# Scores, values and turning of an attention step at one point among the dense products instead of two

## The chip, the cores and the metric

The kernel runs on one core of one Trainium2 chip. The metric is the device time of one execution in microseconds (us); less is better. Engines are named as in the profile: PE is TensorE's matmuls, PEld its weight loads, DVE is VectorE, ACT is ScalarE, POOL is GpSimd, and SP issues DMAs.

## The reference

One decoder layer over 1024 tokens of width 1024, in float32. The input is normalised and multiplied by one wide matrix; the columns feed a sliding-window attention with a sink logit per head, an mLSTM, and several gates; the two branches are projected, gated, summed, projected again and added to the input. What matters here is the attention, with 16 query heads in 4 groups that share a key/value head, and blocks of 128 tokens:

```python
h = rms_norm(x, norm_w)
proj = jnp.einsum('btd,de->bte', h, w_in) + b_in
...
scores = jnp.einsum('bnqkgd,bnskd->bnkgqs', qb, kw).astype(jnp.float32) * (ATTN_HEAD_DIM ** -0.5)
...
probs = jax.nn.softmax(jnp.concatenate([scores, sink], axis=-1), axis=-1)[..., :-1]
out = jnp.einsum('bnkgqs,bnskd->bnqkgd', probs.astype(v.dtype), vw)
```

## The kernel before

**Dense work.** The wide projection is cut into pairs of weight tiles. Each pair costs seven products instead of eight (a Strassen-like scheme), and each product is 12 matmuls of 128x512 (PRODUCT = 12, PAIR = 84), issued at L1036. The weights are split in a high and a low part (ring_hi by ACT at L1396, ring_lo by POOL at L799). A finished product is taken out of PSUM by ACT and DVE in the functions called retire, which wait for it.

**Attention among it.** attention_step(g) handles one group of four heads, g = 0 to 3, and carries 3 pairs, so 252 dense matmuls, with it. Inside it n runs over 0 to 9. Block n's work is spread over three steps:

- scores(n): 8 matmuls at L1123, at the first point of step n;
- turning of block n: 4 transposes of the probabilities at L1172, in step n + 1;
- values of block n: 4 or 8 matmuls at L1165 and L1167, in step n + 2.

The order is written out by hand, engine by engine; semaphores join the engines. PE issues dense matmuls up to a position, then attention work. The positions are

```python
return LEAD + (3 * PAIR - LEAD - TAIL) * (2 * n + half) // (2 * NB + 2)
```

which for half 0 gives 12, 37, 62, 88, 113, 138, 164, 189, 214, 240 for n = 0 to 9, and for half 1 gives 24, 50, 75, 100, 126, 151, 176, 202, 227 for n = 0 to 8.

**The softmax chain of block n.** PE does scores(n). ACT copies the part of the current block to probs (L1596). DVE's combine(n) merges the previous block's part (L2191; L2194 for n = 0), takes the row maxima (L2197, L2200) and gives neg_max (L2203). ACT does four exponentials and the sink's (L1599, L1601). DVE's normalise(n) sums, inverts and scales (L2208, L2210, L2212, and last L2214, which writes probs). PE then turns the block (waits for probs_ready), DVE's select masks the turned block into pT_cur and pT_prev (L2222, L2224), PE multiplies by the values (waits for pT_ready), and for n under 3 ACT copies the result to u_early (L1609), for the others DVE's gate multiplies it into silu_z (L2236).

DVE also does silu of the z gate (L2230) after normalise in steps 4, 5 and 7, and the retired products (L2091 to L2115).

Of the kernel before, what the change touches and what calls it, by code (L numbers as in the profile page):

```python
# [9 lines left out]
ACT = mybir.ActivationFunctionType  # L10
# [3 lines left out]
P = 128  # L14
# [3 lines left out]
NB = T // P  # L18
# [85 lines left out]
def attention_at(n, half):  # L104

    return LEAD + (3 * PAIR - LEAD - TAIL) * (2 * n + half) // (2 * NB + 2)
# [8 lines left out]
def build(nc, x, norm_w, w_in, b_in, sinks, conv_w, conv_b, mnorm_w, wba, wbm, w_out, fnorm_w, out):  # L115
    ctx = ExitStack()
    with ctx:
# [809 lines left out]
        def _(pe):  # L927
# [199 lines left out]
            def attention_step(g):  # L1127
                i0 = 1 + 3 * g
                done = [0]

                def more(hi):

                    pairs(i0, done[0], hi)
                    done[0] = hi

                for n in range(NB + 2):
                    more(attention_at(n, 0))
                    if n < NB:
                        if n == 0:
                            pe.wait_ge(k_in, 32 * (g + 1))  # L1140
                            pe.wait_ge(c11_out, i0)
                            pe.wait_ge(c12_out, i0)
                            if not later(g):
                                pe.wait_ge(g_ready, 1)
                        else:
                            pe.wait_ge(cur_copied, NB * g + n)
                            pe.wait_ge(max_ready, NB * g + n)
                        scores(n).then_inc(scores_done, 1)
                    if n <= NB:
                        more(attention_at(n, 1))  # L1150
                    if n >= 2:
                        m = n - 2
                        pe.wait_ge(pT_ready, NB * g + m + 1)
                        if m == 0:
                            pe.wait_ge(v_in, 16 * (g + 1))
                        if m == 0 and later(g):
                            pe.wait_ge(attn_gated, (NB - EARLY) * g)
                        if 1 <= m <= EARLY:
                            pe.wait_ge(attn_copied, EARLY * g + m)
                        if m > EARLY:  # L1160
                            pe.wait_ge(attn_gated, (NB - EARLY) * g + m - EARLY)
                        for r in range(2):
                            o = ps[64 * r:64 * r + 64, X[3], 0:2 * P]
                            heads = slice(2 * r, 2 * r + 2)
                            mm = nc.tensor.matmul(o, v_head[:, m, :], pT_cur[:, heads, :], start=True, stop=(m == 0))  # L1165
                            if m:
                                mm = nc.tensor.matmul(o, v_head[:, m - 1, :], pT_prev[:, heads, :], start=False, stop=True)  # L1167
                        mm.then_inc(pv_done, 1)
                    if 1 <= n <= NB:
                        pe.wait_ge(probs_ready, NB * g + n)  # L1170
                        for h in range(GR):
                            mm = nc.tensor.transpose(ps[:, X[2], h * P:(h + 1) * P], probs[(n - 1) % 2][:, h, :], ident[:])  # L1172
                        mm.then_inc(probs_turned, 1)
                more(3 * PAIR)
# [170 lines left out]
        def _(act):  # L1345
# [187 lines left out]
            def attention_step(g):  # L1533
# [55 lines left out]
                for n in range(NB + 2):  # L1589
                    retire(attention_at(n, 0))  # L1590
                    if n < NB:
                        pr = probs[n % 2]
                        act.wait_ge(scores_done, NB * g + n + 1)
                        if n >= 2:
                            act.wait_ge(probs_turned, NB * g + n - 1)
                        A(pr[:], both_blocks[:, :, 1, :], ACT.Copy).then_inc(cur_copied, 1)  # L1596
                        act.wait_ge(max_ready, NB * g + n + 1)
                        for h in range(GR):
                            A(pr[:, h, :], pr[:, h, :], ACT.Exp, scale=HD ** -0.5, bias=neg_max[:, h:h + 1],  # L1599
                              accum_out=row_sum[:, h:h + 1])  # L1600
                        A(sink_exp[:], sink_in[:], ACT.Exp).then_inc(exp_ready, 1)  # L1601
                    if n == NB and not final(g, KV):
                        load_k(g + 1)
                    if 2 <= n < EARLY + 2:
                        m = n - 2
                        act.wait_ge(pv_done, NB * g + m + 1)
                        if m == 0:
                            until(act, early_used, g)
                        A(u_early[:, :, m * P:(m + 1) * P], ps[:, X[3], 0:2 * P].rearrange("p (j n) -> p j n", j=2),  # L1609
                          ACT.Copy).then_inc(attn_copied, 1)  # L1610
                    if n <= NB:
                        retire(attention_at(n, 1))
                    if n in (3, 4):
# [379 lines left out]
        def _(dve):  # L1993
# [149 lines left out]
            def attention_step(g):  # L2143
# [94 lines left out]
                for n in range(NB + 2):  # L2238
                    retire(attention_at(n, 0))
                    if n < NB:  # L2240
                        combine(n)
                    if n <= NB:
                        retire(attention_at(n, 1))
                    if 1 <= n <= NB:
                        select(n - 1)
                    if n >= EARLY + 2:
# [1 line left out]
                    if n == NB + 1:  # L2248
                        dve.drain()
                        dve.sem_inc(u_ready, 1)  # L2250
                    if n < NB:
                        normalise(n)
                    if n == 4:
# [415 lines left out]
```

## Time and profile before

| | us |
|---|---|
| median of 3 runs | 1123.01 (1122.79 to 1123.10) |
| the profiled execution | 1122.33 |
| its span in the trace | 1120.6 |
| PE busy | 1100.2 |
| DVE busy | 777.9 |
| ACT busy | 483.3 |
| POOL busy | 641.3 |

The span is what the trace covers; the profiled execution's own time is 1.7 us more. PE is busy nearly all of the span. The four attention groups begin with their first scores at 96, 176, 256 and 336 us. The granted TensorE clock is 0.999 of full speed.

### The profile page before, as it was taken

Reading aid. Unit: us, or ns where it says so; the run is one execution under the profiler, and the core shown is the slowest. Engines: PE = TensorE matmul, PEld = TensorE weight load, DVE = VectorE, ACT = ScalarE, POOL = GpSimd, SP = SyncE. Lnnn points to the kernel's source line nnn. Section 1 sums busy time; section 2 is a strip of 40 time slices with the busy share of each in tenths; the row PEclk is TensorE's granted clock in tenths of the full one; section 3 lists DMA queues with packets and bytes.
Section 4 is the critical chain, followed back from the end, with each engine's and each line's share of the span. In section 5 each row is a group of like instructions: output and inputs, shape, how many; then the busy total and the mean of one; then the engine's idle time right before and its main releaser. Section 6 shows DMA issues by size and latency. Waiting matters only on the chain.

```text
span 1120.6 us, 16419 instructions
## 1 busy us (share of the span) xinstructions
PE 1100.2 (98%) x5363; PEld 877.0 (78%) x5363; DVE 777.9 (69%) x1235; ACT 483.3 (43%) x1134; POOL 641.3 (57%) x441
## 2 busy tenths in 40 slices
PE   6999999999999999999999999999999999999997
PEld 5887777777777778888888888888887888788876
DVE  4966887887878887567756675669578312458897
ACT  7543443534434444454535364545455311131443
POOL 3577455465565469556955695659644434347440
PEclk9999999999999999999999999999999999999999
DMA  6244133142151141112311222122109433853423
GB/s 211 78 86 83 39 94 94 29 117 72 37 149 36 39 136 38 38 39 85 104 38 39 77 88 61 37 75 85 48 20 336 160 104 106 268 167 136 167 93 134
DMA packets 112804, 107.63 MB, mean 96 GB/s; under 512 B 7228, under 2 KB 96696, under 8 KB 111720
## 3 DMA queue, kind: packets, MB, share of 16 engines
q1 hardware_dynamic: 102760, 77.18, 23.2%
q10 hardware_dynamic: 9984, 29.69, 8.5%
q8 instruction: 33, 0.54, 0.2%
q14 instruction: 27, 0.22, 0.1%
HBM read 80.50 MB, written 26.35 MB: 95 GB/s over the span
## 4 chain that ended last, share of the span: by engine, by line
PE 79%; DVE 9%; ACT 4%; DVEq 3%; DMA 2%; issue 2%; ACTq 1%; SPq 0%; POOL 0%; POOLq 0%
PE ps L1036 50%; PE ps L1265 13%; PE ps L942 3%; PE ps L1123 2%; DMA w_raw<-in_w_branch_mlstm 1%; PE ps L1239 1%; PE ps L1223 1%; PE ps L1227 1%; PE ps L1236 1%; PE ps L1165 1%; DVE row_max L2197 1%; PE ps L1172 1%; DVEq L2259 1%; ACT ring_hi L1396 1%; DVE v L2427 1%
## 5 line engine op out<-in xcount | busy, mean ns | idle before, releaser
L799 POOL TENSOR_TENSOR ring_lo<-w,ring_hi 128x512 fp32r<-128x512 f32 x128 | 178.7, 1413 | 136.3 <-ACT ring_hi L1396 136.3
L799 POOL TENSOR_TENSOR ring_lo<-t,ring_hi 128x512 fp32r<-128x512 f32 x96 | 136.3, 1424 | 143.0 <-ACT ring_hi L1396 143.0
L1036 PE MATMUL ps<-s_hi,ring_hi 128*128 128x512 f32 x512 | 203.5, 397 | 0.0
L1036 PE MATMUL ps<-s_lo,ring_hi 128*128 128x512 f32 x512 | 202.6, 396 | 0.0
L1036 PE MATMUL ps<-s_hi,ring_lo 128*128 128x512 f32 x512 | 202.0, 395 | 0.0
L1036 PE MATMUL ps<-h_hi,ring_hi 128*128 128x512 f32 x384 | 152.1, 396 | 0.0
L1036 PE MATMUL ps<-h_hi,ring_lo 128*128 128x512 f32 x384 | 151.9, 396 | 0.0
L1036 PE MATMUL ps<-h_lo,ring_hi 128*128 128x512 f32 x384 | 151.4, 394 | 0.0
L1396 ACT ACTIVATE ring_hi<-w 128x512 fp32r<-128x512 f32 x128 | 75.6, 620 | 93.4 <-PE ps L1036 78.4
L1036 PEld LDWEIGHTS ps<-s_hi,ring_hi 128*128 128x128 f32 x512 | 96.2, 188 | 22.1 <-issue 3.0
L1036 PEld LDWEIGHTS ps<-s_hi,ring_lo 128*128 128x128 f32 x512 | 96.3, 188 | 21.8 <-issue 2.6
L1036 PEld LDWEIGHTS ps<-s_lo,ring_hi 128*128 128x128 f32 x512 | 96.3, 188 | 19.7 <-issue 1.3
L1599 ACT ACTIVATE probs<-probs,neg_max 128x128 f32<-128x128 f32 x128 | 49.9, 391 | 111.2 <-DVE neg_max L2203 111.2
L794 POOL TENSOR_TENSOR t<-w,t 128x512 f32<-128x512 f32 x64 | 94.4, 1475 | 5.1 <-issue 5.1
L782 POOL TENSOR_TENSOR w_hi<-w_raw,zero_col 128x1024 fp32r<-128x1024 f32 (+1 forms) x18 | 37.2, 2065 | 101.2 <-PE ps L1265 58.9
L1036 PEld LDWEIGHTS ps<-h_hi,ring_hi 128*128 128x128 f32 x384 | 72.2, 188 | 16.8 <-issue 1.3
L1036 PEld LDWEIGHTS ps<-h_hi,ring_lo 128*128 128x128 f32 x384 | 72.2, 188 | 15.4 <-issue 1.3
L1036 PEld LDWEIGHTS ps<-h_lo,ring_hi 128*128 128x128 f32 x384 | 72.2, 188 | 15.3 <-issue 1.3
L1396 ACT ACTIVATE ring_hi<-t 128x512 fp32r<-128x512 f32 x96 | 59.3, 623 | 53.8 <-PE ps L1036 46.6
L1265 PE MATMUL ps<-u_a,w_hi 128*128 128x512 f32 x256 | 79.1, 390 | 0.3 <-DVE u_a L2432 0.3
L1814 ACT ACTIVATE ev<-ev 128x1024 f32<-128x1024 f32 x16 | 17.0, 1062 | 110.5 <-DVE merged L2509 49.4
L1265 PE MATMUL ps<-u_m,w_hi 128*128 128x512 f32 x192 | 59.9, 393 | 0.4 <-POOL w_lo L784 0.4
(331 smaller groups left out, 2318.9 us busy)
## 6 DMA issues: line engine op xcount, KB each, us to landing
w<-in_w_in SPq DMA_DIRECT2D x128, 256.0 KB, 3.0
xs<-in_x SPq DMA_DIRECT2D x8, 512.0 KB, 8.3
ga_scratch<-ev ACTq DMA_DIRECT2D x4, 1024.0 KB, 4.8
u_scratch<-silu_z ACTq DMA_DIRECT2D x8, 512.0 KB, 3.4
gm_scratch<-ev ACTq DMA_DIRECT2D x4, 1024.0 KB, 4.8
w_raw<-in_w_branch_attn SPq DMA_DIRECT2D x8, 512.0 KB, 4.1
u_a_f<-u_scratch SPq DMA_DIRECT2D x4, 1024.0 KB, 8.2
ev<-ga_scratch ACTq DMA_DIRECT2D x8, 512.0 KB, 3.5
```

The source lines that it names most:

```text
L782: nc.gpsimd.tensor_tensor(hi, src, zero_col[:].to_broadcast(list(src.shape)), ALU.add)
L794: return nc.gpsimd.tensor_tensor(flat(dst), flat(a), flat(b), op)
L799: return nc.gpsimd.tensor_tensor(flat(lo[:]), flat(raw_or_sum[:]), flat(hi[:]).bitcast(F32), ALU.subtract)
L942: mm = nc.tensor.matmul(ps[:, 2 * s + b, :], w[:, k, :], h[:, k % KH, :], start=(r == 0), stop=(r == KT * TERMS - 1))
L1036: mm = nc.tensor.matmul(ps[:, bank, :], w[:, k, :], h[:, k, :], start=(m == 0), stop=(m == PRODUCT - 1))
L1123: mm = nc.tensor.matmul(o, q_T[rows, j, n * P:(n + 1) * P], k_now[rows, first * P:(n + 1) * P], start=True, stop=True)
L1165: mm = nc.tensor.matmul(o, v_head[:, m, :], pT_cur[:, heads, :], start=True, stop=(m == 0))
L1172: mm = nc.tensor.transpose(ps[:, X[2], h * P:(h + 1) * P], probs[(n - 1) % 2][:, h, :], ident[:])
L1265: mm = nc.tensor.matmul(ps[:, 2 * s + b, :], w[:, k, :], part(k)[(0, 1, 0)[term]][:, token_half(b)], start=(r == 0), stop=(r == KT * TERMS ...
L1396: return A(ring_slot[0][:], raw_or_sum[:], ACT.Copy)
L1599: A(pr[:, h, :], pr[:, h, :], ACT.Exp, scale=HD ** -0.5, bias=neg_max[:, h:h + 1], accum_out=row_sum[:, h:h + 1])
L1814: A(ev[:, j, :], ev[:, j, :], ACT.Tanh, scale=0.5).then_inc(gate_tanh, 1)
```

## The change

On PE the dense matmuls that stood between scores(n) and the values and turning are no longer issued there; they follow in the next step's first run of dense matmuls. So a step has one point for all attention work, at position half 0, and runs of 25 or 26 dense matmuls between the points. ACT's copy of the early values comes ahead of the exponentials, and DVE retires the second product of a step after select and gate.

```diff
--- before.py
+++ after.py
@@ -1146,8 +1146,6 @@
                             pe.wait_ge(cur_copied, NB * g + n)
                             pe.wait_ge(max_ready, NB * g + n)
                         scores(n).then_inc(scores_done, 1)
-                    if n <= NB:
-                        more(attention_at(n, 1))
                     if n >= 2:
                         m = n - 2
                         pe.wait_ge(pT_ready, NB * g + m + 1)
@@ -1594,6 +1592,14 @@
                         if n >= 2:
                             act.wait_ge(probs_turned, NB * g + n - 1)
                         A(pr[:], both_blocks[:, :, 1, :], ACT.Copy).then_inc(cur_copied, 1)
+                    if 2 <= n < EARLY + 2:
+                        m = n - 2
+                        act.wait_ge(pv_done, NB * g + m + 1)
+                        if m == 0:
+                            until(act, early_used, g)
+                        A(u_early[:, :, m * P:(m + 1) * P], ps[:, X[3], 0:2 * P].rearrange("p (j n) -> p j n", j=2),
+                          ACT.Copy).then_inc(attn_copied, 1)
+                    if n < NB:
                         act.wait_ge(max_ready, NB * g + n + 1)
                         for h in range(GR):
                             A(pr[:, h, :], pr[:, h, :], ACT.Exp, scale=HD ** -0.5, bias=neg_max[:, h:h + 1],
@@ -1601,13 +1607,6 @@
                         A(sink_exp[:], sink_in[:], ACT.Exp).then_inc(exp_ready, 1)
                     if n == NB and not final(g, KV):
                         load_k(g + 1)
-                    if 2 <= n < EARLY + 2:
-                        m = n - 2
-                        act.wait_ge(pv_done, NB * g + m + 1)
-                        if m == 0:
-                            until(act, early_used, g)
-                        A(u_early[:, :, m * P:(m + 1) * P], ps[:, X[3], 0:2 * P].rearrange("p (j n) -> p j n", j=2),
-                          ACT.Copy).then_inc(attn_copied, 1)
                     if n <= NB:
                         retire(attention_at(n, 1))
                     if n in (3, 4):
@@ -2239,8 +2238,6 @@
                     retire(attention_at(n, 0))
                     if n < NB:
                         combine(n)
-                    if n <= NB:
-                        retire(attention_at(n, 1))
                     if 1 <= n <= NB:
                         select(n - 1)
                     if n >= EARLY + 2:
@@ -2248,6 +2245,8 @@
                     if n == NB + 1:
                         dve.drain()
                         dve.sem_inc(u_ready, 1)
+                    if n <= NB:
+                        retire(attention_at(n, 1))
                     if n < NB:
                         normalise(n)
                     if n == 4:
```

On PE, at step 1 of a group, the first point at which a block is turned, the difference of the two orders reads as follows (a minus stands before, a plus in the change; L1170 is the old L1172):

```order
 L1123 MATMUL ps<-k_now,q_T 128x256 [waits max_ready,cur_copied]
 L1123 MATMUL ps<-k_now,q_T 128x256 x3
+L1170 MATMUL ps<-ident,probs_159 128x128 [waits probs_ready]
+L1170 MATMUL ps<-ident,probs_159 128x128 x3
 L1036 MATMUL ps<-s_lo,ring_hi 128x512
 L1036 MATMUL ps<-s_hi,ring_lo 128x512
```

The four transposes, with their wait for probs_ready, moved ahead of 13 dense matmuls, to right behind the scores of the next block.

On DVE, in step 4 of the first group, before (ev is the buffer that the retired product goes to):

```order
L2203 TENSOR_SCALAR neg_max<-row_max 128x4
L2096 SCALAR_TENSOR_TENSOR ev<-ps,par,ev 128x512
L2222 TENSOR_TENSOR pT_cur<-ps,cur_T 128x512
L2224 TENSOR_TENSOR pT_prev<-ps,prev_T 128x512
L2208 TENSOR_TENSOR row_inv<-row_sum,sink_exp 128x4
```

and in the same place of the change, whose line numbers are one less:

```order
L2202 TENSOR_SCALAR neg_max<-row_max 128x4
L2221 TENSOR_TENSOR pT_cur<-ps,cur_T 128x512
L2223 TENSOR_TENSOR pT_prev<-ps,prev_T 128x512
L2095 SCALAR_TENSOR_TENSOR ev<-ps,par,ev 128x512
L2207 TENSOR_TENSOR row_inv<-row_sum,sink_exp 128x4
```

The retired product moved behind the two masked copies; both still stand between combine and normalise.

## Rows read from the trace of the kernel before

**Rows 1.** Page, busy us (share of the span) and instructions

```profile
PE 1100.2 (98%) x5363; PEld 877.0 (78%) x5363; DVE 777.9 (69%) x1235; ACT 483.3 (43%) x1134; POOL 641.3 (57%) x441
```

**Rows 2.** Chain that ended last: start us, us, what; first group, step 1

```profile
102.71 1.06 PE ps L1123 x8
103.77 3.17 PE ps L1036 x13
106.95 0.44 PE ps L1172 x4
107.38 2.75 PE ps L1036 x12
```

**Rows 3.** The same view, first group, steps 5 to 8

```profile
145.62 2.94 PE ps L1036 x12
148.56 0.59 PE ps L1165 x4
149.15 0.43 PE ps L1167 x4
149.58 0.59 PE ps L1172 x4
150.17 2.99 PE ps L1036 x13
...
159.00 5.71 PE ps L1036 x25
```

**Rows 4.** Timeline (start us, us, engine, line): scores(1), end of normalise(0)

```profile
102.64 0.73 PEld L1123 LDWEIGHTS ps<-k_now,q_T 64*128 64x128 f32 x8 [0.35 <-issue]
103.43 1.65 DVE L2214 TENSOR_TENSOR probs<-probs,row_inv 128x512 f32<-128x512 f32 x1
```

**Rows 5.** Timeline, second group: scores(1), end of normalise(0), combine(2)

```profile
182.56 0.73 PEld L1123 LDWEIGHTS ps<-k_now,q_T 64*128 64x128 f32 x8 [0.35 <-issue]
184.12 1.78 DVE L2214 TENSOR_TENSOR probs<-probs,row_inv 128x512 f32<-128x512 f32 x1
193.45 0.72 DVE L2191 COPY_PREDICATED probs<-from_prev,ps 128x512 f32<-128x512 int8 x1
```

**Rows 6.** One line's instructions: L2214, duration ns min/median/max

```profile
L2214 DVE TENSOR_TENSOR probs<-probs,row_inv x32: 691/1417/1784, 103.4 to 404.1; 128x512 f32<-128x512 f32 x32
```

**Rows 7.** Timeline: end of normalise(7) in groups 0 to 3

```profile
162.49 1.77 DVE L2214 TENSOR_TENSOR probs<-probs,row_inv 128x512 f32<-128x512 f32 x1
...
242.50 1.78 DVE L2214 TENSOR_TENSOR probs<-probs,row_inv 128x512 f32<-128x512 f32 x1
...
322.32 1.54 DVE L2214 TENSOR_TENSOR probs<-probs,row_inv 128x512 f32<-128x512 f32 x1
...
404.06 1.77 DVE L2214 TENSOR_TENSOR probs<-probs,row_inv 128x512 f32<-128x512 f32 x1
```

**Rows 8.** Timeline, weight loads: values of block 7 in groups 0 to 3

```profile
169.31 0.23 PEld L1165 LDWEIGHTS ps<-pT_cur,v_head 128*64 128x64 f32 x4 [0.41 <-DVE pT_prev L2224]
...
249.36 0.20 PEld L1165 LDWEIGHTS ps<-pT_cur,v_head 128*64 128x64 f32 x4 [0.54 <-DVE silu_z L2236]
...
329.23 0.20 PEld L1165 LDWEIGHTS ps<-pT_cur,v_head 128*64 128x64 f32 x4 [0.35 <-DVE silu_z L2236]
...
410.87 0.23 PEld L1165 LDWEIGHTS ps<-pT_cur,v_head 128*64 128x64 f32 x4 [1.78 <-DVE pT_prev L2224]
```

**Rows 9.** Timeline, weight loads: turning of block 7 in the last group

```profile
405.89 0.42 PEld L1172 LDWEIGHTS ps<-ident,probs 128*128 128x128 f32 x4 [0.67 <-DVE probs L2214]
```

**Rows 10.** Timeline, ACT: around the early copy of step 3, and a copy that PE released

```profile
127.01 0.36 ACT L1609 ACTIVATE u_early<-ps 128x256 f32<-128x256 f32 x1
...
145.67 0.60 ACT L1596 ACTIVATE probs<-ps 128x512 f32<-128x512 f32 x1 [0.69 <-PE ps L1123]
```

**Rows 11.** Timeline, DVE, first group: first instruction of combine(4) and combine(7)

```profile
130.77 0.75 DVE L2191 COPY_PREDICATED probs<-from_prev,ps 128x512 f32<-128x512 int8 x1 [1.60 <-ACT probs L1596]
...
156.41 0.74 DVE L2191 COPY_PREDICATED probs<-from_prev,ps 128x512 f32<-128x512 int8 x1 [0.93 <-ACT probs L1596]
```

## The prediction

> **What bounds the kernel now.** I read the page first: PE is busy 1100.2 of 1120.6 us [rows 1], so any microsecond that PE waits is added and any that it saves is taken off, unless something else holds it. Then the chain of waits inside one attention group, which gives the pitch of PE's work. A run of 25 dense matmuls behind a turning takes 5.71 us, of 13 behind a turning 2.99, of 12 behind scores 2.94 [rows 3]; 13 behind scores take 3.17 and 12 behind the turning of step 1 take 2.75 [rows 2]. Each weight load of scores has 0.35 us of idle before it that nothing released [rows 4]: PE pays for a change between kinds of matmul. Last I read DVE's timeline beside PE's. The last instruction of the softmax chain, L2214, ends shortly before or even after PE wants the block, and in the last group PE already waits 0.67 us for it [rows 9]. So inside a group a second, serial chain runs just ahead of PE: combine, exponentials, normalise, then the next combine. It waits for ACT's copies at places [rows 11], which wait for ACT's own earlier work, and hardly for PE.
>
> **The change, part by part.**
>
> *What PE saves.* In steps 2 to 7 the dense matmuls came in two runs, 12 behind scores and 13 behind a turning: 2.94 + 2.99 = 5.93 us. Now 25 come in one run behind a turning: 5.71 [rows 3]. That is 0.22 us a step, 1.32 for six. In step 1 the old pieces are 1.06 + 3.17 + 0.44 + 2.75 = 7.42 [rows 2], the new ones 1.06 + 0.59 + 5.71 = 7.36, with the 0.59 that a turning takes behind another kind of matmul [rows 3]. Together 1.38 a group, 5.5 us for four. Scores followed directly by values stand nowhere in the trace. I price that boundary as dense to values, which the 0.22 assumes; from below it could cost nothing, from above the idle 0.35 [rows 4] more, 24 times: 8.4 us. I take the middle way of no difference, since below it will turn out that PE isn't what ends a group.
>
> By the idle of 0.35 us alone a group would save six of them and all four 24, 8.4 us. The Trainium skill, TensorEngine Tiling (Array Packing), Key Properties, says that changing the tiling mode drains TensorE; scores, values and dense matmuls have different tile shapes and the change has 24 fewer such switches, so by that rule the change gains. The run lengths above say 0.22 for each rather than 0.35, because the idle is partly time that the pipeline would have taken anyway.
>
> *What PE now waits for: step 1.* The turning of block 0 needs L2214 of normalise(0). It used to stand behind 13 dense matmuls (3.17 us); now it stands directly behind scores(1). In group 0 scores(1) start at 102.64, so PE is free for the turning at 103.70; L2214 ends at 103.43 + 1.65 = 105.08 [rows 4]. With 0.06 us from the end of L2214 (404.06 + 1.77 = 405.83) to the turning (405.89) [rows 7, 9] PE stands 1.44 us. In group 1: free at 182.56 + 1.06 = 183.62, L2214 ends at 184.12 + 1.78 = 185.90 [rows 5], so 2.34 us. Nothing can fill it: PE issues in order, and the dense matmuls are queued behind the turning. Nothing in step 0 is changed on ACT or DVE, so this chain isn't shorter. This alone is more than the 1.38 that a group saves, but it isn't what to add up, for the following reason.
>
> *What ends a group: block 7.* From the turning of block 0 PE alone would need: five runs of 25 with the turning ahead, 0.59 + 5.71 = 6.30 each; two runs of 26 (positions 62 to 88 and 138 to 164), 6.53 each; scores and four value matmuls once, 1.06 + 0.59 = 1.65; scores and eight value matmuls (0.59 + 0.43 = 1.02) five times, 2.08 each; values alone, 1.02, in step 8 [rows 2, 3]. The sum is 31.50 + 13.06 + 1.65 + 10.40 + 1.02 = 57.63. In group 0 that is 105.14 + 57.63 = 162.77 for the turning of block 7. L2214 of normalise(7) ends at 162.49 + 1.77 = 164.26 [rows 7]. So PE waits again, about 1.5 us. In group 1: 185.96 + 57.63 = 243.59 against 244.28: 0.7. In the last group PE waited here already with 13 more dense matmuls ahead [rows 9]. So in every group block 7's L2214 sets the time, and behind it PE now has a run of 26 (214 to 240) where it had 13. The values of block 7 can start 0.06 + 0.59 + 5.94 = 6.59 us behind the end of L2214. (5.94 is 5.71 and one more of 0.23; 0.59 is the turning.)
>
> Against what they do now [rows 7, 8]:
> group 0: 164.26 + 6.59 = 170.85, now 169.31: +1.54;
> group 1: 244.28 + 6.59 = 250.87, now 249.36: +1.51;
> group 2: 322.32 + 1.54 + 6.59 = 330.45, now 329.23: +1.22;
> group 3: 405.83 + 6.59 = 412.42, now 410.87: +1.55.
> The sum is +5.82 us, if DVE's chain from a group's first scores to L2214 of block 7 stays as long as it is.
>
> *Does that chain stay?* DVE's instructions are the same; the retired product of a step only goes behind the masked copies, still between combine and normalise. The product is long finished: in step 7 it ends at position 192, three dense matmuls into a run, and DVE comes to it some 4 us after the turning. Two small terms. ACT's copy of the early values (L1609, 0.36 us [rows 10]; instructions of ACT overlap a little at their ends, and I take 0.27) leaves the stretch between the exponentials and ACT's next copy for a place where ACT waits for DVE. ACT's copy of step 4 is what combine(4) waits for, 1.60 us [rows 11]; so 0.27 off in groups 0, 2, 3. And PE's late turning moves scores(2): in group 1 they start at 185.96 + 6.30 = 192.26, ACT copies 1.18 later (145.67, scores from 144.56 less the 0.07 by which the two views differ [rows 3, 10]; 1.06 of it the scores) and for 0.60, DVE follows 0.15 after: 194.19 against 193.45 now [rows 5], so +0.74 - 0.27 = +0.47 there. In the other groups the same sum comes out before DVE gets there. Together -0.81 + 0.47 = -0.34.
>
> *Edits that cost nothing:* ACT's and DVE's retiring frees PSUM banks three products later, 36 dense matmuls or over 8 us, and moves by 2 us at most; POOL and SP have no line changed. Without that cover a late bank would stop PE at the start of a product, which no row shows now.
>
> **Sum.** 1122.33 (the profiled execution, 0.68 under the median) + 5.82 - 0.34 = 1127.8 us. I leave the 0.68 out.
>
> **Rivals.**
>
> *Forecast: the chain ends each group.* Chance 0.76.
>
> *Faster: PE's saving comes through.* The place is L2214 of block 0 and block 7 in each group. It would have to end 1.4 to 2.3 us earlier in block 0 and 0.7 to 1.5 earlier in block 7. For it: the same instruction on the same shape takes from 0.69 to 1.78 us, median 1.42 [rows 6], so up to 1.1 us of one could go when POOL's work falls elsewhere. Against it: block 0's step is not changed at all, and in group 0 nothing ahead of it is. If all waits vanished the kernel would be 5.5 us faster, 1116.8. It decides from about 1.4 us a group: with less saved than that in waits the gain is gone. Chance 0.06. The Trainium skill, SBUF — State Buffer, Who interferes with whom, says that a VectorE tensor_tensor with both inputs in SBUF contends with GpSimd's reads, one blocking the other; L2214 has both inputs there. No row of mine separates this from other causes of the spread.
>
> *No change: only block 0 waits.* If block 7's chain ends in time, because ACT's copy that combine(7) waits for 0.93 us [rows 11] comes sooner, the waits are those of block 0 only: 1.44 and 2.34 by rows, say 1.3 on average with the other two groups shorter, 5.2 in all, against 5.5 saved: 1122.0. Chance 0.11.
>
> *Worse: the chain gets longer itself.* Each PE wait shifts the next scores, hence ACT's copy, hence combine, as I found in group 1 with 0.74. If that happens in all steps from 1 to 7 with some 0.3 us, a group ends 2 us later than forecast: +8, 1136. Chance 0.07.
>
> **How the numbers follow.** Likeliest 1127.8. The range 1122.5 to 1132.5 reaches down to the case of no change and up over half of the worse case; the bound of L2214, 0.7 us on average to either side in each group, gives 2.8 of it. Two runs differ by 0.03%; 0.2%, 2.2 us, is about what tells a change from none. Faster 0.06, same 0.12, slower 0.82.
>
> **What would show it.** In the profile after: PE's idle put to L2214 (probs_ready) at the turning of block 0 and of block 7 in every group, 1 to 2.5 us each, some 10 us in all; groups' first scores 81 to 82 us apart instead of 80; runs of 25 dense matmuls of 5.71 us; fewer gaps of 0.35. From the last group's end to the end of the span nothing changed. The prediction is wrong if L2214 of block 7 ends at another distance from the group's first scores than now, 68.2 us in group 0, or if scores to values costs PE much more than dense to values.

## The result, and the profile after

The change runs in 1129.44 us (median of 6 runs, 1127.31 to 1131.89), the kernel before in 1123.07 beside it (6 runs, 1122.79 to 1123.97). The ratio is 1.0057, 95% interval 1.0042 to 1.0071: slower by 0.57%. Forecast were 1127.8, with 1122.5 to 1132.5 as the range, and slower with a chance of 0.82. The forecast cost was 5.48 us; the medians differ by 6.4.

The profiled execution of the change took 1131.89 us, the longest of its six, with a span of 1130.2. The page's first line, which answers to [rows 1]:

```profile
PE 1098.2 (97%) x5363; PEld 881.4 (78%) x5363; DVE 777.4 (69%) x1235; ACT 486.8 (43%) x1134; POOL 645.1 (57%) x441
```

PE is busy 2.0 us less in a span that is 9.6 longer. The chain that ended last (start us, us, what) shows what took PE's place in the first group and at the start of the second. L1170 is the turning, L1163 and L1165 are the values, L2213 is the old L2214, L2209 the old L2210:

```profile
106.92 1.65 DVE probs L2213
...
109.27 5.71 PE ps L1036 x25
114.98 1.09 PE ps L1123 x8
...
121.45 1.15 DVE row_inv L2207
...
122.67 1.17 DVE row_inv L2209
...
124.16 1.44 DVE probs L2213
...
126.30 5.70 PE ps L1036 x25
...
165.96 1.77 DVE probs L2213
...
168.43 5.94 PE ps L1036 x26
...
187.53 1.26 DVE row_inv L2209
...
189.11 1.76 DVE probs L2213
...
191.74 7.16 PE ps L1036 x25
```

In [rows 2, 3] the same stretches of the first group were PE's alone. Now DVE's L2213 stands between two runs of dense matmuls, and block 7's, at 165.96, stands right ahead of the run of 26 that leads to the group's end. The last run of 25 shown took 7.16 us where the others take 5.71; the last section comes back to it.

The view of waits at L1170 (engine, line, releaser: us, times, longest):

```profile
PEld ps L1170 <- DVE probs L2213: 17.0, 14, 2.6
...
PE ps L1170 <- DVE probs L2213: 10.9, 13, 2.2
```

The waits over 0.8 us at the weight load are blocks 0 and 7 of the four groups, which were forecast, and block 2 of the four groups (0.85 to 1.23 us) and block 6 of the last (1.38), which weren't. Some of them in the timeline of weight loads:

```profile
108.61 0.42 PEld L1170 LDWEIGHTS ps<-ident,probs 128*128 128x128 f32 x4 [0.99 <-DVE probs L2213]
...
125.64 0.42 PEld L1170 LDWEIGHTS ps<-ident,probs 128*128 128x128 f32 x4 [0.86 <-DVE probs L2213]
...
167.77 0.42 PEld L1170 LDWEIGHTS ps<-ident,probs 128*128 128x128 f32 x4 [1.57 <-DVE probs L2213]
...
190.92 0.42 PEld L1170 LDWEIGHTS ps<-ident,probs 128*128 128x128 f32 x4 [2.62 <-DVE probs L2213]
...
251.30 0.42 PEld L1170 LDWEIGHTS ps<-ident,probs 128*128 128x128 f32 x4 [1.18 <-DVE probs L2213]
...
405.21 0.42 PEld L1170 LDWEIGHTS ps<-ident,probs 128*128 128x128 f32 x4 [1.38 <-DVE probs L2213]
...
413.98 0.42 PEld L1170 LDWEIGHTS ps<-ident,probs 128*128 128x128 f32 x4 [1.85 <-DVE probs L2213]
```

The time is read group by group, from a group's first scores to the values of block 7. First the first scores before, in the timeline of weight loads:

```profile
96.10 0.52 PEld L1123 LDWEIGHTS ps<-k_now,q_T 64*128 64x128 f32 x8 [0.36 <-issue]
...
176.03 0.52 PEld L1123 LDWEIGHTS ps<-k_now,q_T 64*128 64x128 f32 x8 [0.35 <-issue]
...
256.08 0.52 PEld L1123 LDWEIGHTS ps<-k_now,q_T 64*128 64x128 f32 x8 [0.35 <-issue]
...
335.96 0.52 PEld L1123 LDWEIGHTS ps<-k_now,q_T 64*128 64x128 f32 x8 [0.35 <-issue]
```

Then the change, first scores and values of block 7 of the four groups:

```profile
100.31 0.52 PEld L1123 LDWEIGHTS ps<-k_now,q_T 64*128 64x128 f32 x8 [0.36 <-issue]
...
174.30 0.20 PEld L1163 LDWEIGHTS ps<-pT_cur,v_head 128*64 128x64 f32 x4 [0.35 <-issue]
...
181.03 0.52 PEld L1123 LDWEIGHTS ps<-k_now,q_T 64*128 64x128 f32 x8 [0.35 <-issue]
...
257.81 0.20 PEld L1163 LDWEIGHTS ps<-pT_cur,v_head 128*64 128x64 f32 x4 [0.35 <-issue]
...
264.53 0.52 PEld L1123 LDWEIGHTS ps<-k_now,q_T 64*128 64x128 f32 x8 [0.35 <-issue]
...
338.11 0.20 PEld L1163 LDWEIGHTS ps<-pT_cur,v_head 128*64 128x64 f32 x4 [0.35 <-issue]
...
344.83 0.52 PEld L1123 LDWEIGHTS ps<-k_now,q_T 64*128 64x128 f32 x8 [0.35 <-issue]
...
420.49 0.20 PEld L1163 LDWEIGHTS ps<-pT_cur,v_head 128*64 128x64 f32 x4 [0.35 <-issue]
```

Before, the groups took 73.21, 73.33, 73.15 and 74.91 us (values in [rows 8]). Now they take 73.99, 76.78, 73.58 and 75.66: +0.78, +3.45, +0.43, +0.75, together +5.41. From the last values to the end of the span it is 709.73 before and 709.71 now. The remaining 4.2 us of the profiled execution lie ahead of the first scores, where nothing is changed: ACT waited 5.81 us for a store of v (3.01 in the profiled execution of before), POOL for ACT, and PE 2.76 us for POOL's ring_lo, at 95.86. In medians the change is 6.4 us slower, 1.0 more than the groups' +5.41.

The late start reached into the first group. There the maximum of block 0 with the sink, line L2200 before and L2199 in the change, reads in the timeline of DVE, before and then in the change:

```profile
99.69 0.87 DVE L2200 SCALAR_TENSOR_TENSOR row_max<-row_max,sink_tab 128x4 f32<-128x4 f32 x1
...
103.89 0.16 DVE L2199 SCALAR_TENSOR_TENSOR row_max<-row_max,sink_tab 128x4 f32<-128x4 f32 x1
```

Before, it started while a POOL instruction ran (99.25 to 100.55). So L2213 of block 0 ends 8.25 us behind the first scores and not 8.99, though no line of this stretch was changed. Of the twelve traces that have L2213 or its like (no_scale and before_no_scale don't), in two, the change and change_silu_late, PE stood over 2 us just ahead of the first scores, and the distance is 8.25 and 8.27 us; in the ten others it is 8.99 to 9.04. One of these is step8_late (below), the same program up to step 8: 9.01 us, and 68.14 instead of 67.41 to the end of block 7's L2213, while its other three groups repeat the change's within 0.03. So, as an estimate from the two traces, the first group of a usual execution of the change is 0.73 us longer than the profiled one, and the groups' loss +6.14 us, close to the medians' 6.4.

### The profile page after: what moved, and what is told of

Same layout as the page of the kernel before. It is cut to its first block, busy times and chain, and to the rows that moved or that the text cites. A ratio compares the mean times of both kernels' runs of the same rounds, so it can differ in the third digit from the quotient of the medians.

```text
span 1130.2 us, 16419 instructions
## 1 busy us (share of the span) xinstructions
PE 1098.2 (97%) x5363; PEld 881.4 (78%) x5363; DVE 777.4 (69%) x1235; ACT 486.8 (43%) x1134; POOL 645.1 (57%) x441
## 4 chain that ended last, share of the span: by engine, by line
PE 67%; DVE 16%; ACT 5%; DMA 4%; DVEq 4%; issue 3%; ACTq 1%; POOL 0%; SPq 0%; POOLq 0%
PE ps L1036 43%; PE ps L1263 13%; DVE probs L2213 2%; DVE row_max L2196 1%; DMA w_raw<-in_w_branch_mlstm 1%; DVE probs L2190 1%; PE ps L1237 1%; PE ps L1221 1%; DVE row_inv L2209 1%; PE ps L1225 1%; PE ps L1234 1%; ACT ring_hi L1394 1%; DMA v_scratch<-v_stage 1%; ACT probs L1594 1%; ACT probs L1605 1%
## 5 line engine op out<-in xcount | busy, mean ns | idle before, releaser
L799 POOL TENSOR_TENSOR ring_lo<-w,ring_hi 128x512 fp32r<-128x512 f32 x128 | 181.3, 1435 | 148.2 <-ACT ring_hi L1394 148.2
```

The source lines that it names most:

```text
L799: return nc.gpsimd.tensor_tensor(flat(lo[:]), flat(raw_or_sum[:]), flat(hi[:]).bitcast(F32), ALU.subtract)
```

## The experiments

All times are medians; the ratio is against the kernel before, run beside them (medians 1123.24, 1123.07, 1123.07). "Groups" is what the four groups of the profiled execution took, less the 294.60 of before.

| kernel | us | ratio [95%] | groups |
|---|---|---|---|
| the change | 1129.44 | 1.0057 [1.0042, 1.0071] | +5.41 |
| step1_late | 1127.40 | 1.0035 [1.0021, 1.0048] | +5.07 |
| step8_late | 1123.84 | 1.0004 [0.9995, 1.0013] | +1.92 |
| values_early | 1121.92 | 0.9986 [0.9977, 0.9995] | -1.48 |
| no_scale | 1114.92 | 0.9923 [0.9910, 0.9937] | -8.19 |
| before_no_scale | 1120.78 | 0.9982 [0.9973, 0.9991] | -2.01 |
| orders_only | 1127.56 | 1.0045 [1.0031, 1.0058] | +3.00 |
| values_early_silu_late | 1119.49 | 0.9970 [0.9960, 0.9980] | -3.70 |
| change_silu_late | 1125.35 | 1.0020 [1.0011, 1.0029] | +1.75 |
| dve_order_only | 1126.46 | 1.0029 [1.0018, 1.0040] | +2.60 |
| act_order_only | 1123.36 | 1.0002 [0.9993, 1.0011] | +0.15 |
| pe_and_act_order | 1132.47 | 1.0082 [1.0068, 1.0096] | +9.82 |
| pe_order_only | 1130.36 | 1.0059 [1.0045, 1.0073] | +7.54 |

The groups and the medians agree within 1.5 us everywhere, mostly within 1. The groups are one execution, and the two executions with the late start (the change, change_silu_late) show 0.73 us too little in the first. orders_only and dve_order_only lose another 1.5 and 1.1 us behind the last values (711.22 and 710.82 us to the end, against 709.73).

**Step 1 undone (step1_late).** If the wait at block 0 is itself the cost, this gives it back; if block 7's chain ends the group, it gives nothing. The diff is against the change, as are all but where it is said.

```diff
                         scores(n).then_inc(scores_done, 1)
+                    if n in (1,):
+                        more(attention_at(n, 1))
...
                         combine(n)
+                    if n in (1,):
+                        retire(attention_at(n, 1))
```

> The change with one step undone: in step 1 the turning of block 0 stands behind 13 dense matmuls again. Theory A (a group ends when block 7's L2214 ends, which hangs on the serial chain of ACT and DVE alone): PE's wait of 1.0 to 2.6 us for block 0 goes, but the wait for block 7 grows by nearly as much; only the slow stretch behind the long wait of the second group (about 1.6 us in the profiled run) and its late scores(2) go. 1126 to 1128 us. Rival B (PE's waits add up, each on its own): the waits for block 0 are taken off and the others stay as they are, 1129.4 - 5.7 - 1.6 = about 1122 us.

Measured 1127.40; the groups stay at +5.07. The wait went one block on, in the timeline of weight loads:

```profile
115.04 0.42 PEld L1172 LDWEIGHTS ps<-ident,probs 128*128 128x128 f32 x4 [1.99 <-DVE probs L2215]
...
166.49 0.42 PEld L1172 LDWEIGHTS ps<-ident,probs 128*128 128x128 f32 x4 [1.60 <-DVE probs L2215]
```

115.04 is block 1 and 166.49 block 7. The four groups take 75.18, 74.43, 73.98 and 76.08 us, against 73.99, 76.78, 73.58 and 75.66 in the change. So the third and fourth are 0.4 us longer without the wait at block 0, and the first too when its late start is allowed for: there that wait isn't what costs. In the second it is, by 2.35 us, since the wait of 2.22 us brings the slow run of 7.16 us with it (last section); here PE's waits stay at 1.54 us and less in the groups, and the clock at 1.00. That this slow stretch would go is what theory A expected. The waits for block 7, which it expected to grow, are the same within 0.1 us; the waits stand at block 1 instead (0.77 to 1.54 us of PE's idle).

**Step 8 undone (step8_late).** The same edit with `n in (8,)`: the values of block 7 are then 13 dense matmuls behind its turning, not 26.

> The change with one step undone: in step 8 the values of block 6 and the turning of block 7 stand behind 13 dense matmuls again, so behind the turning there is a run of 13, not 26. The waits for block 0 stay. Theory A: block 7's L2214 ends when it did, but 13 fewer dense matmuls (3.0 us) stand behind it; the next values then wait for DVE's gate of block 6 and come about 5.0 us behind the end of L2214 instead of 6.6: 1.5 us a group, about 6 us off the change, 1122.5 to 1124.5 us. Rival B: PE only waits less for block 7, by its 1.2 to 1.8 us in each group, and pays one more gap: 1124 to 1126 us; rival C (block 0 is what counts): hardly below the change, 1128 to 1130 us.

Measured 1123.84. In the first group block 7's turning (166.70) and values (170.27) wait for nothing:

```profile
166.70 0.42 PEld L1172 LDWEIGHTS ps<-ident,probs 128*128 128x128 f32 x4 [0.39 <-issue]
170.27 0.21 PEld L1165 LDWEIGHTS ps<-pT_cur,v_head 128*64 128x64 f32 x4 [0.35 <-issue]
```

In the four groups the values of block 7 come 5.38, 5.79, 5.82 and 5.05 us behind the end of L2215 instead of 6.56 to 6.59: 4.3 us less in all, not the 6 of theory A, and they don't wait for the gate, as it had thought. The median falls by 5.6 of the 6.4 us; the 1.3 between isn't traced. All waits for block 0 are still there (1.79 and 2.63 us in the first two groups). What is left in the groups, +1.92, comes from the second (+2.68); the other three together are 0.76 us shorter than before.

**Scores and values together, turning apart (values_early).** One boundary less on PE, and the turning keeps 12 to 13 dense matmuls behind the scores; DVE in the order of before.

```diff
                         mm.then_inc(pv_done, 1)
+                    if n <= NB:
+                        more(attention_at(n, 1))
                     if 1 <= n <= NB:
                         pe.wait_ge(probs_ready, NB * g + n)
```

(and DVE's second retire back ahead of select)

> Scores and values stand at the first point of a step, the turning alone at the second; ACT's early copy ahead of the exponentials as in the change, DVE's retiring where it was before. The L2214 of a block has its old 13 dense matmuls of cover again, and a turning between dense runs pays no gap. By PE's pieces a step costs 1.06 + 1.02 + 3.17 + 0.44 + 2.75 = 8.44 us instead of 8.59: 3.6 us off before in all, 1119.5, if PE alone counts (rival B). Theory A: PE's waits of the change vanish, but a group still ends with DVE's chain, which is as long as before: 1121.5 to 1123.5 us, with PE's idle at the values of block 7 grown instead.

Measured 1121.92, a little faster than before, and in theory A's range. The values of block 7 wait instead of its turning, as in the second group here, which keeps part of PE's saving from coming through:

```profile
249.09 0.20 PEld L1163 LDWEIGHTS ps<-pT_cur,v_head 128*64 128x64 f32 x4 [1.04 <-DVE silu_z L2237]
```

**The chain shortened (no_scale, before_no_scale).** Both leave out the scaling of the probabilities by row_inv; no_scale does so in the change, before_no_scale in the kernel before.

```diff
-                    V.reciprocal(row_inv[:], row_inv[:])
-                    dve.drain()
-                    V.tensor_tensor(pr[:], pr[:], row_inv[:].unsqueeze(2).to_broadcast([P, GR, P]), ALU.mult)\
-                        .then_inc(probs_ready, 1)
+                    V.reciprocal(row_inv[:], row_inv[:]).then_inc(probs_ready, 1)
```

> The change with L2213, the last instruction of normalise, left out: the probabilities aren't scaled, and probs_ready comes from the reciprocal ahead of it. The serial chain is 0.7 to 1.8 us shorter for each of eight blocks. Theory A: nearly all waits of PE at the turning vanish and PE's saving comes through: 1116.5 to 1118.5 us, 5 to 6 us below before. Rival D (what the change costs lies on PE itself, at the new boundary from scores to values, or in dense runs that are longer): the time stays above before, 1126 us or more.

> The kernel before with L2214, the last instruction of normalise, left out: the probabilities aren't scaled. By the before trace PE waits for the chain of DVE only about 4 us in all (groups' ends), so Theory A: 1118.5 to 1121.5 us, and the change with the same left out (1114.92) stays below it by the 5.5 us that its shorter PE work was priced at, or by 4 to 6. Rival D (the change costs PE itself something): 1114.9 or less.

1114.92 and 1120.78. With the chain 0.7 to 1.8 us shorter in each block, the order of the change is 5.9 us faster than that of before. Its groups took 71.60, 71.60, 71.60 and 71.61 us: PE alone sets them. Those of before_no_scale took 73.15, 73.14, 73.15 and 73.15. So the change saves PE 1.55 us a group, 6.2 in all, and loses it to the chain. This leaves no room for a cost on PE itself at the new boundary. no_scale is 1.6 us under the expected range: PE saves 0.7 us more than I had priced, and the 2.0 us of waits that the groups of before still have (294.60 against 292.59) go as well.

**ACT's and DVE's new orders without PE's (orders_only).** Here the positions on PE are those of before.

```diff
                         scores(n).then_inc(scores_done, 1)
+                    if n <= NB:
+                        more(attention_at(n, 1))
```

> The order of ACT and DVE of the change, PE's order of before. Theory A: nothing that PE waits for in a step moves by more than some 0.3 us; DVE's masked copies come 0.7 to 1.5 us ahead of where they were, but must wait for the turning at the second point: 1121.5 to 1124.5 us. If ACT's or DVE's new order were the cause, it would lie near the change's 1129.

The expectation failed: 1127.56, 4.5 us slower than before by orders that I had called free. Two groups of lines of orders_only (line engine op, count; busy, mean ns; idle before, releaser):

```profile
L2223 DVE TENSOR_TENSOR pT_cur<-ps,cur_T 128x512 f32<-128x512 f32 x32 | 22.0, 686 | 3.2 <-PE ps L1172 3.0
...
L2211 DVE TENSOR_SCALAR row_inv<-row_inv 128x4 f32<-128x4 f32 x32 | 18.8, 586 | 2.9 <-issue 0.6
```

DVE now waits 3.0 us for the turning ahead of the masked copies, and the short multiplication of row_inv takes 586 ns in the mean; before, the same line took

```profile
L2210 DVE TENSOR_SCALAR row_inv<-row_inv 128x4 f32<-128x4 f32 x32 | 13.2, 413 | 2.9 <-issue 0.6
```

**The two orders one by one.** dve_order_only, act_order_only and orders_only have PE's order of before, pe_order_only and pe_and_act_order that of the change. The edit in question on DVE is

```diff
-                    if n <= NB:
-                        retire(attention_at(n, 1))
                     if 1 <= n <= NB:
                         select(n - 1)
...
+                    if n <= NB:
+                        retire(attention_at(n, 1))
                     if n < NB:
                         normalise(n)
```

> The kernel before with DVE's order alone: the second product of a step is retired behind the masked copies and the gate. The orders of ACT and DVE together cost 4.5 us on PE's old order, which I had not expected; in its trace the masked copies wait 3.0 us in all for the turning and L2211, a short tensor_scalar, takes 18.8 us in all instead of 13.2. If DVE's order is the cause: 1126 to 1128 us. If ACT's early copy is: 1122.5 to 1123.5 us here.

> The kernel before with ACT's order alone: the early copy of steps 2 to 4 comes ahead of the exponentials and waits for values that PE's old order gives only at the second point. If DVE's order is the cause of the 4.5 us: 1122.5 to 1124 us here; if this wait is: 1125 to 1127.5 us.

> The change with DVE's order of before: the second product of a step is retired ahead of the masked copies. With PE's new order a turning is long done when DVE comes to the masked copies, so the wait that DVE's order costs on PE's old order can't be there, and by theory A only how L2213's and L2209's long forms fall can differ: 1126 to 1130 us. If DVE's order costs its 3 to 4 us here too, 1124.5 to 1126 us.

> The change on PE alone, ACT and DVE as before. Theory A: the same chain ends each group: 1126.5 to 1130.5 us, within 1.5 us of the version with ACT's order too, since that moves one copy of 0.36 us by some 2 us. If the change's cost came from ACT's or DVE's orders: at most 1124 us.

ACT's order changes nothing on PE's old order (1123.36). DVE's alone costs 3.4 us there (1126.46), so it is most of what made orders_only slow. On PE's new order it is the other way: without it the change is at 1132.47, 3.0 us slower than with it, and above both ranges expected. Without both orders it is at 1130.36, 2.1 us from that, where at most 1.5 was expected. So the edits don't add up: PE's alone costs 7.3 us, ACT's on top of it 2.1 more, and DVE's on top of both gives 3.0 back, though it costs 3.4 us by itself.

The traces show where. In pe_and_act_order the multiplication of row_inv in block 5 takes 1.28 to 1.31 us in the last three groups; in the change, in pe_order_only and before it takes 0.17 in all four. Second group, timeline of POOL and DVE, first pe_and_act_order, then pe_order_only:

```profile
228.07 1.29 POOL L799 TENSOR_TENSOR ring_lo<-w,ring_hi 128x512 fp32r<-128x512 f32 x1 [8.23 <-ACT ring_hi L1394]
228.08 1.31 DVE L2209 TENSOR_SCALAR row_inv<-row_inv 128x4 f32<-128x4 f32 x1
...
228.17 0.17 DVE L2208 TENSOR_SCALAR row_inv<-row_inv 128x4 f32<-128x4 f32 x1
228.22 1.29 POOL L799 TENSOR_TENSOR ring_lo<-w,ring_hi 128x512 fp32r<-128x512 f32 x1 [8.22 <-ACT ring_hi L1394]
```

It starts 0.01 us behind POOL's instruction in the one and 0.05 ahead of it in the other. From L2213 of block 4 to L2213 of block 5 pass 10.02 us in these three groups of pe_and_act_order and 8.80, 8.78 and 8.78 in the change, 3.7 us in all; that is what DVE's new order wins back there, and why ACT's earlier copy costs there. The same instruction of block 5 takes 1.14 to 1.28 us in the last three groups of dve_order_only, and 1.10 to 1.16 in all four of orders_only. This is read from traces; no run moved POOL's work alone.

**silu moved (change_silu_late, values_early_silu_late).** silu(3) stands in step 7 behind normalise(7), ahead of the masked copies of block 7. It goes one step later, behind them and the gate, with one drain more (a wait of DVE for its own earlier instructions).

```diff
-                    if n in (5, 7):
+                    if n in (5, 8):
+                        dve.drain()
                         silu(2 if n == 5 else 3)
```

> The change with the same move of silu(3). Theory A: PE waits for L2213 of block 7, ahead of this silu, and behind it a run of 26 dense matmuls covers what follows: no gain, 1127 to 1130.5 us. If instead DVE's total work were the bound, it would change nothing either; if the chain behind L2213 of block 7 mattered, some 4 us off, 1125 us.

> Scores and values at the first point, the turning at the second, and silu(3), 1.7 us of DVE that stood between L2214 of block 7 and the masked copies of block 7, moved to behind the gate of step 8. Theory A: PE's waits for the values of block 7, 0.6 us over the usual gap in three groups and 0.2 in one, vanish, about 2 us: 1119 to 1120.5 us, the fastest. Rival: the silu is paid for elsewhere, 1121.5 to 1123 us as without the move.

values_early_silu_late is the fastest kernel: 1119.49, ratio 0.9970 [0.9960, 0.9980]. Its first three groups take 72.32 us each, 0.72 more than the order of the change when nothing makes it wait. It beats both kernels.

change_silu_late came out lower than expected, at 1125.35, near the "1125" of the rival that block 7's chain behind L2213 matters; but the time isn't gained there. Of the groups' fall from +5.41 to +1.75, 3.2 us lie in the second group, at block 0, ahead of any silu of that group. The timeline of DVE and POOL there, first in the change:

```profile
187.53 1.26 DVE L2209 TENSOR_SCALAR row_inv<-row_inv 128x4 f32<-128x4 f32 x1 [0.43 <-issue]
...
187.50 1.26 POOL L799 TENSOR_TENSOR ring_lo<-t,ring_hi 128x512 fp32r<-128x512 f32 x1 [3.87 <-ACT ring_hi L1394]
```

and with silu moved:

```profile
186.49 0.17 DVE L2209 TENSOR_SCALAR row_inv<-row_inv 128x4 f32<-128x4 f32 x1
...
186.82 1.27 POOL L799 TENSOR_TENSOR ring_lo<-t,ring_hi 128x512 fp32r<-128x512 f32 x1 [3.88 <-ACT ring_hi L1394]
186.99 1.64 DVE L2213 TENSOR_TENSOR probs<-probs,row_inv 128x512 f32<-128x512 f32 x1
...
188.69 0.42 PEld L1170 LDWEIGHTS ps<-ident,probs 128*128 128x128 f32 x4 [1.07 <-DVE probs L2213]
```

In the change an idle of 0.43 us that nothing released makes L2209 start 0.03 us behind POOL's instruction, and it takes 1.26 us, as long as POOL's. Without that idle it is done before POOL starts, and takes 0.17. PE's wait is 1.07 instead of 2.62, and the clock doesn't fall behind it. The idle stands at this instruction in the traces of all kernels with silu(3) in step 7 and the scaling in place, ten of them, and in neither of the two with silu moved; no_scale and before_no_scale don't have it either. Counted along DVE's instructions in the trace, it stands at the 320th in the change. Idles of 0.45 and 0.43 us stand at the 192nd (L2199) and the 448th (L2213). With silu moved the 320th is L2207, where DVE waits 1.02 us for ACT anyway, and the 448th is L2211, again with 0.43 us of idle. So it goes by the place in the stream of instructions and not by the work that stands there. What happens at these places isn't shown.

## Why the prediction was right

**The mechanism held.** Block 7's chain ends each group. Behind the end of its L2213 the values of block 7 come 6.58, 6.57, 6.59 and 6.56 us later, where 6.59 was forecast. Undoing step 1 makes three groups no shorter, undoing step 8 shortens all, and with a shorter chain PE's saving comes through in full. The forecast wait for block 0 was there: 1.44 and 2.34 us forecast, 0.59 and 2.22 of PE's own idle measured, and 1.39 us in the first group of step8_late, whose start was not late. As the prediction put it, it is not what to add up, but for the second group, where it also slowed the clock; that the prediction didn't have.

**The sum held, in part by luck.** The groups were forecast at +5.82 - 0.34 = +5.48 and measured at +5.41. By group:

| group | forecast | measured |
|---|---|---|
| 0 | +1.54 - 0.27 = +1.27 | +0.78 |
| 1 | +1.51 + 0.47 = +1.98 | +3.45 |
| 2 | +1.22 - 0.27 = +0.95 | +0.43 |
| 3 | +1.55 - 0.27 = +1.28 | +0.75 |

The term that was off is "does that chain stay?". From a group's first scores to the end of L2214 of block 7 it was 68.16, 68.25, 67.78 and 69.87 us before [rows 7], and is 67.41, 70.21, 66.99 and 69.10 now: -0.75, +1.96, -0.79, -0.77 where I had -0.27, +0.47, -0.27, -0.27. The two errors cancel, which is luck. By the prediction's own sign, that it is wrong if this distance changes, the term failed; it had itself forecast small changes of it.

In group 1 what is missing is the stretch at half the clock ahead of scores(2): a run of 25 dense matmuls in 7.16 instead of 5.71 us, and the turning ahead of it in 0.82 instead of 0.59. In step1_late, where the clock doesn't fall, this group's distance is 67.85.

In groups 2 and 3 ACT's early copy is there as priced: from L2213 of block 3 to that of block 4 pass 8.34 and 8.31 us instead of 8.60 and 8.59. Another 0.5 us is gone between block 0 and block 3 (23.00 instead of 23.47, and 23.39 instead of 23.86), for which I had no term. It isn't that L2213 got shorter. L2213 took 38.3 us in all instead of 42.1, block 1's in each group at 0.69 us and not 1.65 to 1.67; but L2207 and L2209 took 25.2 instead of 21.1. It hangs on PE's order in step 1: pe_order_only has about half of it (23.27 us in group 2), pe_and_act_order all (23.01), and step1_late none (23.43). How it comes about stays open. In group 0 the same 0.5 is there too (23.00 instead of 23.48), the late start took 0.74 more, and 0.52 came back between blocks 3 and 4; without the late start the distance would be as before (68.14 in step8_late).

**PE's saving** was priced at 1.38 us a group and is 1.55. The boundary from scores to values, which no row had shown, costs about what dense to values was taken to cost: in the first group scores(2) start at 114.91, the values at 115.98, with 0.33 us of idle at the weight load. The upper bound of +8.4 us didn't come. The Trainium skill's rule on a changed tiling mode (TensorEngine Tiling (Array Packing), Key Properties) points the right way, and 6.2 us for 24 switches fewer is 0.26 each, nearer to the 0.22 of the run lengths than to the idle of 0.35.

**Wrong: DVE's order "costs nothing".** I looked at whether its instructions stay between the same two neighbours and at free PSUM banks. dve_order_only and pe_and_act_order show a price of 3.4 us on PE's old order and a gain of 3.0 on the new. What was left out is where DVE's short instructions fall against POOL's. Against pe_order_only, which has neither of the two orders, the change is only 0.9 us faster, so the sum didn't show it. DVE's order on PE's new one without ACT's wasn't run.

**What would show it.** PE's own idle at the turnings of blocks 0 and 7 was forecast at some 10 us and is 8.0 (0.59, 1.12, 2.22, 0.73, 0.65, 0.70, 0.63 and 1.40); the 10.9 of the view of waits hold blocks 2 and 6 as well. First scores were to be 81 to 82 us apart and are 80.72, 83.50 and 80.30, so none is in that range; the mean is. Nothing changed after the last group (709.73, 709.71). Of the median's +1.0 beyond the groups the late start explains some 0.7 us, by the estimate above; the rest is small beside the spread of the six runs (1127.31 to 1131.89).

## What to carry to other kernels

Where PE issues in order among dense work, the distance between two steps of a serial chain is a resource: merging points saves PE a switch each, but every dependence that now stands at one point needs a whole run to cover it. Compute, for the last block of the chain, the end of the chain plus the run behind it, and compare that with the saving; then undo the merge only where the chain is short of cover. Here undoing it in step 8 only got back to the time of before (1123.84 against 1123.24), and keeping the turning apart gained 1.3 us on it (1121.92). And an order that moves no work can still cost or give 3 us, if it shifts a short instruction in the chain by a few hundredths of a us, from just ahead of POOL's instruction to just behind it.

## What the runs showed of the hardware

**The granted clock after a wait of PE.** In the change PE stood 2.22 us ahead of the turning at 190.92. The stretches that follow (busy us and count of PE, PEld, DVE, ACT, POOL; granted clock; DMA share; GB/s):

```profile
190.00:192.00 2.00, 1.08 (x6) 0.98 (x7) 2.00 (x3) 0.00 (x0) 1.84 (x3) 0.82 0.00 0
192.00:194.00 2.00, 2.00 (x6) 1.61 (x5) 1.77 (x6) 0.39 (x2) 1.24 (x2) 0.50 0.00 0
194.00:196.00 2.00, 2.00 (x9) 1.54 (x9) 0.36 (x2) 1.36 (x9) 0.00 (x0) 0.83 0.00 0
196.00:198.00 2.00, 2.00 (x10) 1.67 (x9) 1.69 (x5) 0.00 (x0) 0.00 (x0) 1.00 0.00 0
```

0.50 is the 1.2 GHz level, and 1.00 the 2.4 GHz level. Single matmuls of the timeline show it: at the low level

```profile
192.39 0.63 PE L1036 MATMUL ps<-s_hi,ring_hi 128*128 128x512 f32 x1
192.82 0.63 PE L1036 MATMUL ps<-s_lo,ring_hi 128*128 128x512 f32 x1
```

0.43 apart, and 0.23 apart again from 194.84 on. It costs 7.16 - 5.71 = 1.45 us in this run of 25. From 20 us to the end of the last group the fourteen traces hold six waits of PE over 2 us, and the clock is at 0.50 behind each: 2.76 us at 95.86 and 2.22 at 190.92 in the change, 2.10 at 95.10 in change_silu_late, 2.23 at 186.91 in step8_late, 2.22 at 188.22 in pe_and_act_order and 2.22 at 187.84 in pe_order_only. Behind shorter waits it stayed at 1.00 every time in that stretch; ahead of 20 us orders_only and values_early_silu_late have one fall each without a wait over 1.75 us just before it. They reach up to 1.74 us (step1_late, at 94.88) and 1.59 us (block 7 in pe_and_act_order's second group). The Trainium skill, TensorE: Matmul & The Clock Gate, Part 1, has activity decide the clock; these rows agree: the 2.22 us in which PE did nothing came right before the fall. So this wait was dearer than its length.

**DVE beside POOL.** In the traces of both kernels and of the ten experiments that keep the scaling, I sorted every instruction of five kinds in the four groups by whether a POOL instruction was running when it started:

| DVE instruction | POOL running at its start | POOL free |
|---|---|---|
| multiplication of row_inv, 128x4, SBUF | 113, all 1.09 to 1.31 us | 271, all 0.17 us |
| scaling of probs, 128x512, both inputs SBUF | 268, all 1.04 to 1.79 | 116, all 0.69 |
| masked copy, 128x512, one input PSUM | 166, all 0.67 to 0.69 | 554, the same |
| row maximum, one input SBUF | 180, all 0.69 | 204, the same |
| copy of the previous block's part, 128x512, from PSUM | 236, all 0.72 to 0.75 | 100, the same |

For the first two the split has no exception, and the last three don't feel POOL at all. The multiplication ends 0.02 to 0.03 us behind POOL's instruction all 113 times, so it takes what POOL's has left. The addition ahead of it (L2208 before, 128x4, two inputs in SBUF) isn't in the table: it started beside POOL 97 times and ended 0.02 to 0.03 us behind it in 92, for up to 1.28 us. Of the other five, which took their usual 0.15 to 0.16, four started within 0.01 us of POOL's instruction and one just before its end. The Trainium skill, SBUF — State Buffer, Who interferes with whom, says that VectorE instructions with two inputs in SBUF contend with GpSimd instructions that read SBUF, that tensor_scalar can in its two-port modes, and that outside those modes instructions with at most one input in SBUF don't, nor tensor_reduce; the traces agree in each row of the table. In the prediction I had left this rule aside because "no row of mine separates this from other causes of the spread"; counting the starts does separate them, and could have been done on the trace of before. No run took POOL's work away, so what the kernel would gain without the contention was not tried.
